# Conditioned decoder layer in fp32 on one core: the conditioning vector is loaded first and the sum of squares moves into the modulation

## The chip, the cores and the metric

The kernel runs on 1 core of one Trainium2 chip. The metric is the device time of one execution in microseconds (us); the median of three runs of the kernel before is 2164.31 us. Five engines matter here: TensorE (PE) multiplies, VectorE (DVE), ScalarE (ACT) and GpSimd (POOL) do elementwise work, SyncE (SP) issues most of the loads. SP and ACT each feed one hardware DMA queue; both queues are served by the same 16 DMA engines.

## The reference, cut to what matters

One layer for 320 tokens (256 of a prompt, 8 samples of 8 tokens), width 4096, weights in float32. The part that the change touches is the head of it:

```
mod = c @ w_ada + b_ada                       # c: 9 conditioning vectors of 4096, w_ada: 4096 x 12288
shift, scale, gate = split(mod, 3)
h = x * rsqrt(mean(x*x) + EPS) * g_norm * (1 + scale) + shift
proj = h @ w_in                               # then convolutions, RG-LRU, S5, GLU
x = x + gate * (mixed @ w_out)                # and a final RMSNorm
```

So each group of 4 x 128 channels of h needs three things: 1/rms of x (one number per token, over all 4096 channels), that group's shift, and that group's scale.

## The kernel before, in words

Each engine runs one program, ordered by semaphores; there is no scheduler. Everything is channel-major: x is held as 32 tiles of 128 channels x 320 tokens (5 MB).

**The modulation.** `w_ada` comes in slabs of 512 KB (two 128 x 512 tiles). 16 slabs make one part (512 output columns: shift or scale), two parts make one group j, and the first four groups (8 parts, 128 slabs) are worked through before the first projection: this is `with pe.Fori(0, ADA_1)`, lines 404 to 411. For each slab `ada_slab` (line 393) multiplies it by `c`, which is the stationary operand (CT, 32 columns). One slab shows as 4 MATMUL records of line 393. After a part, ACT copies the sums out of PSUM (`acc_copy`, line 576), and PE turns them to channel-major by `ada_sum` (line 401). Slab numbers in this document count from 0 over the whole stage: part 0 of group 0 is slabs 0 to 15, its part 1 slabs 16 to 31.

**The ring.** SP loads the slabs into a ring of 8 slots: 8 at once (line 299), and then slab n as soon as PE has used slab n - 8 (`ada_used`, line 303). After the 120th refill SP issues the first four slabs of `w_in` (line 307) and the next ring of `w_ada` (line 313).

**The sum of squares.** ACT issues x first and then 13 small loads on its own queue (lines 539 to 548), among them c, and six of these share the semaphore `small_in`. When all are issued ACT squares x in 8 pieces (line 555), DVE adds them up (lines 850, 853), and PE sums over the partitions with four matmuls against ones (line 386), 8 records in the trace. PE does this first of all; the modulation stands behind it in PE's program.

**The chain behind the sum.** ACT takes the root (line 559), then begins the preparation of the S5 coefficients together with DVE: exp (563), products (860, 861), exp (565), softplus and range reduction (864 to 872), exp (568), two sines (570, 571), and on DVE the softplus series (876 to 885). Only behind these stands DVE's reciprocal that makes 1/rms (line 888, `rstd_done`). In ACT's program `acc_copy` of group 0 stands behind the two sines. PE's program waits for `rstd_done` at the end of part 0 of every group, ahead of `ada_sum`, and no slab of part 1 is used before that:

```
                    if part == 0:
                        pe.wait_ge(rstd_done, 1)
                    ada_sum(j, part)
```

DVE goes on with the S5 preparation up to line 918 (`bb_ready`), then makes the first group of h (lines 927 to 944, with ACT's line 580). `ada_sum` of group j also waits until h of group j - 1 is written (`ht_done`).

**After the stage.** The projections follow, 3 matmuls of 320 columns per weight tile (lines 375 to 377), in 56 blocks, with the rest of `w_ada` between them; then the recurrences, the output projection and the final norm. Nothing there is touched by the change.

Of the kernel before, what the change touches and what calls it, by code (L numbers as in the profile page):

```python
# [30 lines left out]
T = TP + DB * DS  # L31
# [8 lines left out]
SPG = KT // 2  # L40
# [18 lines left out]
ADA_1 = ADA_J // 2  # L59
# [45 lines left out]
def build(nc, a):  # L105
    ctx = ExitStack()
    with ctx:
        def sem(name):

            return ctx.enter_context(nc.semaphore(name))  # L110
# [4 lines left out]
        def at(name, off, *shape, dt=F32):  # L115
            n = int(np.prod(shape))
            assert off + n <= WORDS, name
            t = nc.alloc_sbuf_tensor_at(name, [P, *shape], dt, offset=ORIGIN + 4 * off)
            return t
# [3 lines left out]
        def take(n):  # L123
            nonlocal o
            start = o
            o += -(-n // 8) * 8
            return start
# [16 lines left out]
        CT = at("c_T", o_ct, KT, 32)  # L144
        PAR = at("par", take(N_PAR), N_PAR)
        SELONES = at("sel_ones", take(9 + P), 9 + P)
        SEL, ONES = SELONES[:, 0:9], SELONES[:, 9:9 + P]
        o_s5h0 = take(512)
        S5H0 = at("s5_h0", o_s5h0, NST, 2, DB)
        o_cb = take(384)  # L150
        CBST = at("convb_state", o_cb, 16, DB, 3)
        LRU0 = at("lru_h0", take(128), 16, DB)
# [15 lines left out]
        SQA = at("x_sqa", o_h + 14 * REP + 8 * T, 4 * T)  # L168
# [68 lines left out]
        A0 = [ctx.enter_context(nc.psum_tensor(f"aux{i}", [P, 512], F32)) for i in range(4)]  # L237
# [6 lines left out]
                          for k, n, width in (("part_c", 2, SW), ("part_b", 4, XW)))  # L244


        small_in, x_in, s5_in = sem("small_in"), sem("x_in"), sem("s5_in")
        w_landed = [sem(f"w_landed{i}") for i in range(RING)]
        ada_landed = [sem(f"ada_landed{i}") for i in range(2 * RING)]
        adax_landed = [sem(f"adax_landed{i}") for i in range(RING)]  # L250
# [5 lines left out]
        sq_done, sqa_done, sum_done, root_done, rstd_done = map(  # L256
            sem, ["sq_done", "sqa_done", "sum_done", "root_done", "rstd_done"])
# [102 lines left out]
        def _(pe):  # L360
            mm = nc.tensor.matmul
# [18 lines left out]
                last.then_inc(slab_done, 1)  # L380


            pe.wait_ge(small_in, 16 * 6)
            pe.wait_ge(sqa_done, 8)
            for i in range(4):
                last = mm(A0[3][:, 0:T], ONES, SQA[:, i * T:(i + 1) * T], start=i == 0, stop=i == 3)  # L386
            last.then_inc(sum_done, 1)

            def ada_slab(part, sl, slot):
                for kk in range(2):  # L390
                    k = 2 * sl + kk
                    r = 32 * (k % 4)
                    last = mm(A0[part][r:r + 32, :], CT[:, k, :], slot[:, kk, :], start=k < 4, stop=k >= KT - 4)  # L393
                last.then_inc(ada_used, 1)

            def ada_sum(j, part):

                pe.wait_ge(acc_out, 2 * j + part + 1)
                pe.wait_ge(ht_done, j + 1)
                for b in range(BLK):  # L400
                    last = mm(A0[2 + part][:, 9 * b:9 * b + 9], ACCS[:, b * P:(b + 1) * P], SEL, start=True, stop=True)
                last.then_inc(sel_done, 1)

            with pe.Fori(0, ADA_1) as j:
                for part in range(2):
                    for sl in range(SPG):
                        pe.wait_ge(ada_landed[sl % 8], 64 * j + 32 * part + 16 * (sl // 8 + 1))
                        ada_slab(part, sl, ADA[:, sl % 8])
                    if part == 0:
                        pe.wait_ge(rstd_done, 1)  # L410
                    ada_sum(j, part)


            with pe.Fori(0, ADA_J - ADA_1) as jj:
# [18 lines left out]
            with pe.Fori(0, N_A) as u:  # L433
                for c in range(SPG):
                    slab(SLAB_A + u * SPG, c, KT, Q_A + u, H_HI, H_LO, T)
                    if c in (1, 3, 6, 9):
                        j = c // 3
# [4 lines left out]
                        for n in range(2):  # L442
# [3 lines left out]
                            last = mm(out, BBU_LO[r, n, :], UU_HI[r, :], start=False, stop=True)  # L446
                        last.then_inc(bu_done, 1)
                    if c in (8, 15):
# [5 lines left out]
                        for n in range(2):  # L454
                            for par in range(2):
                                j = 2 * pair + par
                                last = mm(A0[2][32 * j:32 * j + 32, 0:SW], CC[:, n, j, :], HRI[par][:, n, :],
                                          start=n == 0, stop=n == 1)
# [9 lines left out]
            with pe.Fori(0, N_B // 2) as i:  # L468
                for c in range(SPH):
                    slab(SLAB_B + i * SPB, c, KT // 2, Q_B + 2 * i, H_HI, H_LO, T, k0=KT // 2)  # L470
                for c in range(SPG):
                    slab(SLAB_B + i * SPB + SPH, c, KT, Q_B + 2 * i + 1, H_HI, H_LO, T)
                    if c in (5, 11):
# [5 lines left out]
                        for hd in range(2):  # L479
                            for w in range(2):  # L480
                                last = mm(A0[2 * w + hd][:, 0:XW], WG[:, 2 * pr + hd, w, :],  # L481
                                          XB[:, 2 * pr + hd, :], start=True, stop=True)
# [5 lines left out]
            with pe.Fori(0, N_O) as j:  # L488
                n = 0
                for c in range(SPG):  # L490
# [3 lines left out]
                    for _ in range(per[c]):  # L494
                        pe.wait_ge(gate_landed[n % RING], 64 * j + 16 * (n // RING + 1))
                        for kk in range(2):
                            k = 2 * n + kk
                            r = 32 * (k % 4)
                            last = mm(A0[0][r:r + 32, :], CT[:, k, :], ADA2[:, n % RING, kk, :], start=k < 4,  # L499
                                      stop=k >= KT - 4)  # L500
                        last.then_inc(gate_used, 1)
                        n += 1
                    if c == 13:
                        pe.wait_ge(gacc_out, j + 1)
                        pe.wait_ge(gmod_done, j + 1)
                        for b in range(BLK):
                            last = mm(A0[1][:, 9 * b:9 * b + 9], ACC2[:, b * P:(b + 1) * P], SEL, start=True,
                                      stop=True)
# [6 lines left out]
        def _(act):  # L515
# [20 lines left out]
                    act.wait_ge(slab_done, nb_next + 1)  # L536


            act.dma_start(X[:], a["x"]).then_inc(x_in, 16)
            for dst, name in ((CT, "c"), (PAR, "par"), (SELONES, "sel_ones"), (S5H0, "s5h0"), (LRU0, "lru"),  # L540
                              (CAST, "ca")):
                act.dma_start(dst[:], a[name]).then_inc(small_in, 16)
            for i in range(3):
# [19 lines left out]
            fn(T0[2][:], T0[2][:], ACT.Exp).then_inc(s5_act, 1)  # L563
            act.wait_ge(s5_dve, 2)
            fn(T0[6][:], T0[6][:], ACT.Exp).then_inc(s5_act, 1)
            act.wait_ge(small_in, 16 * 6)
            act.wait_ge(s5_dve, 3)
            fn(NEG8SP[:], NEG8SP[:], ACT.Exp).then_inc(s5_act, 1)
            act.wait_ge(s5_dve, 4)
# [67 lines left out]
            with act.Fori(0, 2) as h:  # L637
                st.enter(h, 32)
                for m in range(4):
# [3 lines left out]
                    for c in range(AHEAD, AHEAD + SPG):  # L643
# [8 lines left out]
                        if c in (3, 6, 9, 12):  # L652
                            j = c // 3 - 1
# [10 lines left out]
                        if c in (6, 9, 12, 15):  # L664
                            j = c // 3 - 2
# [145 lines left out]
            for g in range(FIN_DVE, ADA_J):  # L811
                for b in range(BLK):
                    k = 4 * g + b
                    act.wait_ge(fin_pool, k - 4 * FIN_DVE + 1)
                    last = fn(X[:, k, :], X[:, k, :], ACT.Copy, scale=PAR[:, C_GF + k:C_GF + k + 1])
# [4 lines left out]
        def _(dve):  # L820
# [15 lines left out]
            def col(c):  # L836

                return PAR[:, bass.ds(c, 1)] if not isinstance(c, int) else PAR[:, c:c + 1]
# [20 lines left out]
            dve.wait_ge(s5_act, 1)  # L859
            tt(ANG[:], IM[:], DT[:], MUL)  # L860
            tt(MAG[:], RE[:], DT[:], MUL).then_inc(s5_dve, 1)
            dve.wait_ge(small_in, 16 * 6)
            lam = PAR[:, C_LAM:C_LAM + 16]
            then(ts(SPT[:, 0], lam, -1.0, None, MUL))
            then(tt(SPT[:, 1], SPT[:, 0], lam, ALU.max))
# [315 lines left out]
            for g in range(FIN_DVE):  # L1181
                for b in range(BLK):
                    k = 4 * g + b
                    last = stt(X[:, k, :], X[:, k, :], col(C_GF + k), RST2[:], MUL, MUL)  # L1184
# [243 lines left out]
```

## Time and profile before

| | |
|---|---|
| median of 3 runs | 2164.31 us (2162.28 to 2164.57) |
| span of the profiled execution | 2165.0 us |
| PE busy over the span | 2033.5 us (94%) |
| DVE, ACT, POOL busy | 1053.5, 801.1, 437.0 us |
| first matmul of the program | 37.42 us |
| first matmul of the modulation | 41.82 us |
| last slab of the stage | 201.10 us |

The page gives the span only; no own time of the profiled execution beside it is listed. Its span lies 0.7 us above the median of the runs, so nothing that matters lies outside it. All moments below are microseconds from the start of the span. In the timeline a row is start, duration, engine, line, what, count, and in brackets how long the engine was idle before and what released it.

### The profile page before, as it was taken

The numbers are of one execution on the slowest core, as the hardware profiler recorded it, in microseconds if no ns is written. First come the engines' busy times: TensorE is split into PE (matmuls) and PEld (weight loads), VectorE is DVE, ScalarE is ACT, GpSimd is POOL, SyncE is SP. The second block draws the span as 40 slices with busy tenths as digits, with TensorE's granted clock in tenths as the row PEclk, the third lists the DMA queues.
The fourth block names the chain that finished last, engine by engine and source line by source line (L and its number), as shares of the span: only waits on it lengthen the run. The fifth ranks groups of instructions, "written<-read, shape, count | busy, mean of one in ns | idle before, by whom it ended". The sixth has DMA issues, their size and how long they took to land.

```text
span 2165.0 us, 36787 instructions
## 1 busy us (share of the span) xinstructions
PE 2033.5 (94%) x13066; PEld 1729.1 (80%) x13066; DVE 1053.5 (49%) x1324; ACT 801.1 (37%) x1075; POOL 437.0 (20%) x501
## 2 busy tenths in 40 slices
PE   2787999999999998999988999999999999999994
PEld 0112777778999988899988999999978887888883
DVE  4812233334446787666876456555643333333234
ACT  3001232233244444444444464745733222333222
POOL 0000000000008765687657000000000000000001
PEclk9999999999999999999999999999999999999997
DMA  8999999997443333433334535444386678666862
GB/s 319 410 410 378 339 340 354 339 336 281 148 146 129 129 109 126 134 128 128 120 120 139 171 129 177 152 153 170 107 322 219 227 273 301 231 222 223 300 223 97
DMA packets 129150, 473.89 MB, mean 219 GB/s; under 512 B 14640, under 2 KB 15472, under 8 KB 128960
## 3 DMA queue, kind: packets, MB, share of 16 engines
q1 hardware_dynamic: 122256, 445.70, 57.6%
q0 software_dynamic: 4816, 18.10, 2.4%
q10 hardware_dynamic: 2016, 9.42, 1.1%
q8 instruction: 20, 0.33, 0.1%
q14 instruction: 42, 0.34, 0.1%
HBM read 463.09 MB, written 10.07 MB: 219 GB/s over the span
## 4 chain that ended last, share of the span: by engine, by line
PE 75%; POOL 7%; DMA 7%; issue 4%; DVE 4%; ACTq 1%; ACT 1%; POOLq 0%; SPq 0%; DVEq 0%
PE m L375 22%; PE m L377 21%; PE m L376 21%; DMA ada_ring<-in_ada 6%; PE aux L499 4%; PE aux L393 4%; POOL s_tmpp L1257 1%; POOL s_tmpp L1260 1%; PE aux L481 1%; POOL sin L1216 1%; DVE x L1184 1%; POOL s_h__105 L1256 1%; POOL cos L1218 1%; DMA ada_ring_x<-in_ada 1%; DVE w_lo L833 1%
## 5 line engine op out<-in xcount | busy, mean ns | idle before, releaser
L375 PE MATMUL m<-h_hi,w_hi 128*128 128x320 f32 x3584 | 1134.8, 317 | 4.8 <-DVE w_lo L833 4.8
L377 PE MATMUL m<-h_hi,w_lo 128*128 128x320 f32 x3584 | 1110.0, 310 | 0.0
L376 PE MATMUL m<-h_lo,w_hi 128*128 128x320 f32 x3584 | 1109.6, 310 | 0.0
L833 DVE TENSOR_TENSOR w_lo<-w_raw,w_hi 128x1024 fp32r<-128x1024 f32 x456 | 578.8, 1282 | 866.0 <-ACT w_hi L529 864.9
L529 ACT ACTIVATE w_hi<-w_raw 128x1024 fp32r<-128x1024 f32 x456 | 479.4, 1057 | 929.3 <-PE m L377 604.9
L375 PEld LDWEIGHTS m<-h_hi,w_hi 128*128 128x128 f32 x3584 | 675.5, 188 | 150.6 <-issue 126.2
L376 PEld LDWEIGHTS m<-h_lo,w_hi 128*128 128x128 f32 x3584 | 676.0, 189 | 0.8
L377 PEld LDWEIGHTS m<-h_hi,w_lo 128*128 128x128 f32 x3584 | 675.4, 188 | 0.0
L393 PE MATMUL aux<-ada_ring,c_T 128*32 128x512 f32 x512 | 121.9, 613 | 24.7 <-DMA ada_ring<-in_ada 24.7
L393 PEld LDWEIGHTS aux<-ada_ring,c_T 128*32 128x32 f32 x512 | 17.5, 108 | 122.8 <-DMA ada_ring<-in_ada 119.3
L499 PE MATMUL aux<-gate_ring,c_T 128*32 128x512 f32 x512 | 93.1, 605 | 1.7 <-DMA gate_ring<-in_ada 1.7
L393 PE MATMUL aux<-ada_ring_x,c_T 128*32 128x512 f32 x512 | 70.3, 612 | 3.6 <-DMA ada_ring_x<-in_ada 3.6
L1309 POOL DMA_DIRECT2D x<-in_x x8 | 4.3, 534 | 330.5 <-PE m L377 330.5
L1226 POOL DMA_DIRECT2D part_b<-part_b x4 | 2.4, 590 | 339.5 <-ACT part_b L605 339.5
L1313 POOL TENSOR_TENSOR x<-x,rstd 128x320 f32<-128x320 f32 x8 | 8.6, 1111 | 235.9 <-DVE rstd L1179 235.9
L1300 POOL COPY stage_h<-lru_r 128x18 f32<-128x18 f32 x8 | 4.9, 616 | 240.7 <-DVE lru_r L1094 240.7
L576 ACT ACTIVATE ada_acc<-aux 128x512 f32<-128x512 f32 x16 | 9.5, 594 | 115.9 <-PE aux L393 115.9
L1256 POOL TENSOR_TENSOR s_h__104<-q,cos 128x328 f32<-128x328 f32 x16 | 19.7, 1233 | 155.1 <-DVE q L1007 155.1
L1219 POOL TENSOR_TENSOR sin<-sin,cos 128x328 f32<-128x328 f32 x34 | 43.4, 1278 | 6.0 <-POOL cos L1218 5.9
L628 ACT ACTIVATE cos<-sin 128x328 f32<-128x328 f32 x33 | 15.7, 475 | 70.7 <-POOL sin L1219 70.6
L386 PE MATMUL aux<-x_sqa,sel_ones 128*128 128x320 f32 x8 | 4.5, 740 | 37.4 <-DVE x_sqa L853 37.4
L1260 POOL TENSOR_TENSOR s_tmpp<-q,cos 128x328 f32<-128x328 f32 x32 | 36.3, 1136 | 0.0
(237 smaller groups left out, 1520.4 us busy)
## 6 DMA issues: line engine op xcount, KB each, us to landing
w_raw<-in_w SPq DMA_DIRECT2D x456, 512.0 KB, 4.3
ada_ring<-in_ada SPq DMA_DIRECT2D x128, 512.0 KB, 9.0
ada_ring_x<-in_ada SPq DMA_DIRECT2D x128, 512.0 KB, 5.9
gate_ring<-in_ada SPq DMA_DIRECT2D x128, 512.0 KB, 5.2
x<-in_x ACTq DMA_DIRECT2D x1, 5120.0 KB, 16.6
x<-in_x POOLq DMA_DIRECT2D x8, 640.0 KB, 5.9
out_y<-x SPq DMA_DIRECT2D x7, 640.0 KB, 2.9
part_b<-part_b POOLq DMA_DIRECT2D x4, 688.0 KB, 6.2
```

The lines of the kernel that those rows point to most:

```text
L375: mm(out, w_hi, hi[:, k, :], start=k == k0, stop=False)
L376: mm(out, w_hi, lo[:, k, :], start=False, stop=False)
L377: last = mm(out, w_lo, hi[:, k, :], start=False, stop=k == k0 + nk - 1)
L393: last = mm(A0[part][r:r + 32, :], CT[:, k, :], slot[:, kk, :], start=k < 4, stop=k >= KT - 4)
L481: last = mm(A0[2 * w + hd][:, 0:XW], WG[:, 2 * pr + hd, w, :], XB[:, 2 * pr + hd, :], start=True, stop=True)
L499: last = mm(A0[0][r:r + 32, :], CT[:, k, :], ADA2[:, n % RING, kk, :], start=k < 4, stop=k >= KT - 4)
L529: fn(W_HI[:, c % RING], RAW[:, c % RING].rearrange("p (k n) -> p k n", k=2), ACT.Copy).then_inc(w_hi_done, 1)
L833: tt(W_LO[:, c % RING], RAW[:, c % RING].rearrange("p (k n) -> p k n", k=2), W_HI[:, c % RING].bitcast(F32), SUB).then_inc(w_lo_done, 1)
L1184: last = stt(X[:, k, :], X[:, k, :], col(C_GF + k), RST2[:], MUL, MUL)
L1219: tt(sin, sin, cos, SUB).then_inc(frac_done, 1)
L1256: tt(hr, qr, cos, MUL)
L1260: then(tt(TMPP[:], qi, cos, MUL))
```

## The change

PE no longer begins with the sum of squares. c is loaded first on ACT's queue and has a semaphore of its own; PE waits for it and starts on slab 0. The first of the four groups is written out ahead of the loop (now over groups 1 to 3), and in it, behind slab 13 of part 0, PE waits for the small loads and for the last addition of squares, and does the four matmuls with ones. Nothing else moves; the chain behind the sum is the same.

```
-            pe.wait_ge(small_in, 16 * 6)
-            pe.wait_ge(sqa_done, 8)
-            for i in range(4):
-                last = mm(A0[3][:, 0:T], ONES, SQA[:, i * T:(i + 1) * T], start=i == 0, stop=i == 3)
-            last.then_inc(sum_done, 1)
+            def x_sum():
+
+                pe.wait_ge(small_in, 16 * 5)
+                pe.wait_ge(sqa_done, 8)
+                for i in range(4):
+                    last = mm(A0[3][:, 0:T], ONES, SQA[:, i * T:(i + 1) * T], start=i == 0, stop=i == 3)
+                last.then_inc(sum_done, 1)
...
-            with pe.Fori(0, ADA_1) as j:
+            def ada_alone(j, first):
                 for part in range(2):
                     for sl in range(SPG):
                         pe.wait_ge(ada_landed[sl % 8], 64 * j + 32 * part + 16 * (sl // 8 + 1))
                         ada_slab(part, sl, ADA[:, sl % 8])
+                        if first and part == 0 and sl == SPG - 3:
+                            x_sum()
                     if part == 0:
                         pe.wait_ge(rstd_done, 1)
                     ada_sum(j, part)
+
+            pe.wait_ge(c_in, 16)
+            ada_alone(0, True)
+            with pe.Fori(1, ADA_1) as j:
+                ada_alone(j, False)
...
+            act.dma_start(CT[:], a["c"]).then_inc(c_in, 16)
             act.dma_start(X[:], a["x"]).then_inc(x_in, 16)
-            for dst, name in ((CT, "c"), (PAR, "par"), (SELONES, "sel_ones"), (S5H0, "s5h0"), (LRU0, "lru"),
+            for dst, name in ((PAR, "par"), (SELONES, "sel_ones"), (S5H0, "s5h0"), (LRU0, "lru"),
                               (CAST, "ca")):
```

The waits of ACT and DVE on `small_in` go from six loads to five as well.

## Rows read from the trace of the kernel before

**Rows 1.** The page: the span in 40 slices, of 54 us each.

```profile
PEclk9999999999999999999999999999999999999997
DMA  8999999997443333433334535444386678666862
```

**Rows 2.** Stretches: us, busy time of PE, PEld, DVE, ACT, POOL, then PEclk, DMA share, GB/s.

```profile
30.00:35.00 5.00, 0.00 (x0) 0.00 (x0) 4.69 (x4) 4.03 (x4) 0.00 (x0) 1.00 1.02 408
35.00:40.00 5.00, 2.58 (x5) 1.82 (x6) 2.17 (x2) 1.68 (x2) 0.00 (x0) 1.00 0.12 43
40.00:45.00 5.00, 5.00 (x36) 1.64 (x35) 0.11 (x1) 2.90 (x3) 0.00 (x0) 1.00 0.16 51
...
60.00:80.00 20.00, 15.86 (x68) 2.68 (x67) 19.76 (x14) 0.60 (x1) 0.00 (x0) 0.91 1.03 409
```

**Rows 3.** Timeline, 20 to 60 us: from ACT's last issue to slab 16.

```profile
20.88 1.54 ACTq L548 DMA_DIRECT2D s_step<-in_step  x1
...
37.42 4.46 PE L386 MATMUL aux<-x_sqa,sel_ones 128*128 128x320 f32 x8 [37.42 <-DVE x_sqa L853]
...
41.82 3.64 PE L393 MATMUL aux<-ada_ring,c_T 128*32 128x512 f32 x32
41.93 0.53 ACT L559 ACTIVATE rstd<-aux,eps 128x320 f32<-128x320 f32 x1 [5.23 <-PE aux L386]
...
51.21 1.05 PE L393 MATMUL aux<-ada_ring,c_T 128*32 128x512 f32 x4 [0.21 <-DMA ada_ring<-in_ada]
...
56.34 1.05 PE L393 MATMUL aux<-ada_ring,c_T 128*32 128x512 f32 x4 [0.22 <-DMA ada_ring<-in_ada]
...
56.98 2.15 DVE L888 RECIPROCAL rstd<-rstd 128x320 f32<-128x320 f32 x1
57.52 0.60 ACT L576 ACTIVATE ada_acc<-aux 128x512 f32<-128x512 f32 x1 [1.56 <-PE aux L393]
...
59.37 1.05 PE L401 MATMUL aux<-sel_ones,ada_acc 128*128 128x9 f32 x8 [1.98 <-DVE rstd L888]
60.35 2.19 PE L393 MATMUL aux<-ada_ring,c_T 128*32 128x512 f32 x16
```

**Rows 4.** Timeline, 60 to 215 us: slab 27, first h, last slab, end of stage.

```profile
73.10 1.05 PE L393 MATMUL aux<-ada_ring,c_T 128*32 128x512 f32 x4 [0.23 <-DMA ada_ring<-in_ada]
...
96.44 1.27 ACT L580 ACTIVATE h_hi<-h_tmp 128x1280 f32 x1 [16.44 <-DVE h_tmp L941]
...
99.89 0.60 ACT L576 ACTIVATE ada_acc<-aux 128x512 f32<-128x512 f32 x1 [2.18 <-PE aux L393]
...
201.10 1.05 PE L393 MATMUL aux<-ada_ring,c_T 128*32 128x512 f32 x4 [0.23 <-DMA ada_ring<-in_ada]
...
207.50 3.17 PE L393 MATMUL aux<-ada_ring_x,c_T 128*32 128x512 f32 x8 [3.59 <-DMA ada_ring_x<-in_ada]
```

**Rows 5.** DMA issues, 0 to 60 us: KB each, median us from issue to landing.

```profile
x<-in_x ACTq DMA_DIRECT2D x1, 5120.0 KB, 16.6
c_T<-in_c ACTq DMA_DIRECT2D x1, 512.0 KB, 18.7
```

**Rows 6.** DMA queues, 0 to 60 us: packets, MB, share (q1 is SP's, q10 ACT's).

```profile
q10 hardware_dynamic: 2016, 9.42, 39.6%
```

**Rows 7.** DMA issues, 2.1 to 2.2 us, 6.2 us, and 42.0 to 43.3 us.

```profile
ada_ring<-in_ada SPq DMA_DIRECT2D x1, 512.0 KB, 15.8
ada_ring<-in_ada SPq DMA_DIRECT2D x1, 512.0 KB, 24.9
ada_ring<-in_ada SPq DMA_DIRECT2D x1, 512.0 KB, 3.2
```

**Rows 8.** DMA queues, 2.5 to 10 us, then 17.5 to 25 us.

```profile
q10 hardware_dynamic: 65, 2.66, 84.6%
q1 hardware_dynamic: 40, 0.16, 5.3%
...
q1 hardware_dynamic: 621, 2.28, 74.9%
q10 hardware_dynamic: 615, 0.79, 28.6%
```

**Rows 9.** Stretches around the two times that PE stands still.

```profile
66.00:68.00 2.00, 2.00 (x10) 0.21 (x6) 1.93 (x3) 0.00 (x0) 0.00 (x0) 0.50 1.04 414
205.00:210.00 5.00, 2.50 (x8) 0.38 (x8) 4.59 (x10) 1.28 (x2) 0.00 (x0) 0.55 0.59 234
```

**Rows 10.** The chain that ended last: start, us, what; eight full-clock fp32 records.

```profile
1260.22 2.31 PE aux L481 x8
```

More of the change, by code:

```diff
@@ L244, in build @@
                           for k, n, width in (("part_c", 2, SW), ("part_b", 4, XW)))
-        small_in, x_in, s5_in = sem("small_in"), sem("x_in"), sem("s5_in")
+        small_in, c_in, x_in, s5_in = sem("small_in"), sem("c_in"), sem("x_in"), sem("s5_in")
         w_landed = [sem(f"w_landed{i}") for i in range(RING)]
@@ L565, in _ @@
             fn(T0[6][:], T0[6][:], ACT.Exp).then_inc(s5_act, 1)
-            act.wait_ge(small_in, 16 * 6)
+            act.wait_ge(small_in, 16 * 5)
             act.wait_ge(s5_dve, 3)
@@ L861, in _ @@
             tt(MAG[:], RE[:], DT[:], MUL).then_inc(s5_dve, 1)
-            dve.wait_ge(small_in, 16 * 6)
+            dve.wait_ge(small_in, 16 * 5)
             lam = PAR[:, C_LAM:C_LAM + 16]
```

## The prediction

> **What bounds the kernel now.** I read the page first, slice by slice: the DMA engines are nine tenths busy or more through the first four slices, about 216 us, and only half busy later [rows 1]. So the head of the kernel, where `w_ada` streams in, is set by the loads, and the rest by TensorE. Whatever the change does, it does in the head; what follows depends on it through one moment only, the end of the stage, and shifts with it as a block.
>
> Then the stretches of the head. The loads run at 408 GB/s to 35 us, nearly stop for two stretches (share 0.12 and 0.16), and run at full share afterwards [rows 2]. The hole is 5 x 0.88 + 5 x 0.84 = 8.6 us. The timeline says why: all 8 ring slots are full, PE does not touch them before 41.82 us because the sum of squares stands ahead in its program, starts at 37.42 and takes 4.46 us, and ACT could only begin to square when its last issue was out at 22.42 us (20.88 + 1.54) [rows 3]. This hole is what the change can win.
>
> The same timeline shows a second place. PE stands still at the end of part 0 until line 401 at 59.37, released by the reciprocal of line 888 [rows 3]. That reciprocal ends a chain which begins when the sum is done, at 37.42 + 4.46 = 41.88. The chain is therefore 59.37 - 41.88 = 17.5 us long. In the kernel before PE needs 57.4 us for its first 16 slabs anyway (56.34 + 1.05), so only 2 us of the chain are seen. From slab 27 at 73.10 to slab 127 at 201.10 it is 128.0 us for 100 slabs, 1.28 us each, every one released by its load [rows 4]: in this stretch a shift at slab 27 arrives whole at the end of the stage.
>
> **The change part by part.** One slab is 0.524 MB, 1.28 us.
>
> *c ahead of x, own semaphore.* c landed 18.7 us after its issue because it stood behind x; x took 16.6 us for 5 MB [rows 5]. Now c lands within a few us and x about 1.3 us later (0.52 MB at 408 GB/s). Neither is on the path: PE's first slab landed at about 2.1 + 15.8 = 17.9 us, also behind x [rows 7]. The reason is in the queues: from 2.5 to 10 us ACT's queue moved 2.66 MB in 65 packets and SP's only 0.16 MB in 40 [rows 8], so x with its 41 KB packets takes nearly everything. PE will begin at about 18 us, not at 4. The squares end at about 37.4 us, within 1.5 us of before, since ACT's issues are paced by the same queue; they are needed only behind slab 13. Cost 0; if that cover went, a late square would delay the chain one for one, and it has some 7 us to spare.
>
> *Modulation first.* As slab 0 is used at about 19 us, the refills follow at once and the hole at 36 us closes: slab 8 need not wait until 43. Gain to that point 8.6 us.
>
> *When is slab 13 there?* Before, 9.42 MB of ACT's queue [rows 6] and 8 slabs (4.19 MB) were through at about 35.6 us (the 0.12 of the stretch from 35 us) [rows 2]. Six slabs more are 3.15 MB, 7.7 us at 408 GB/s: 43.3 us. About 1 us goes from last byte to use, and the last small loads (0.3 MB, 0.8 us) may come behind: 44.0 us. Bounds: 45 us if all small loads win; and 40.2 us if SP's queue kept the 75% share of the stretch from 17.5 to 25 us [rows 8] from slab 0 on (18 + 13 x 0.524 / 0.306). I take 44.0: after that stretch ACT's queue carries rows of 4 KB like SP's own, and the two should share about evenly.
>
> On this point the Trainium skill (DMA: Bandwidth & Descriptors, Queues, rings and completion order) says that each DMA engine goes round the queues that have work, one packet at a time. The trace agrees for x (41 KB against 4 KB a turn, shares 84.6% and 5.3%) [rows 8]; by that rule slab 13 comes at 44, while a constant 75% share would put it at 40.2 and the forecast 3.8 us lower.
>
> A second rule speaks against the sum. The Trainium skill (same page, Specifications) gives 358 GB/s as the limit of HBM for one core. By it the 3.15 MB would take 8.8 us, and the forecast would be 1.1 us higher; the trace has 408 to 414 GB/s over whole stretches [rows 2, 9], and the measurement decides.
>
> *The sum inside the stage.* Behind slab 13 (44.0 + 1.0 for its matmuls) stand the 8 records. Before they ran after 37 us of idleness and took 4.46 us [rows 3]; eight fp32 records of a little more columns take 2.31 us in a busy stretch [rows 10], so the former is the 1.2 GHz level. In the stretch from 66 us the clock was 0.50 after PE had been standing and starting again [rows 9], so either level is possible here. I take 2.3, with 4.5 as upper bound, because the slabs now keep PE working from 18 us on. The sum is done at 44.0 + 1.0 + 2.3 = 47.3 us, 5.4 us later than before. The 2.3 us themselves are covered by the ring.
>
> *The chain behind it* is unchanged in work and order: 17.5 us. All its other inputs are there by then. `ada_sum` of part 0 starts at 47.3 + 17.5 = 64.8 us, not 59.37, and slab 16 at 64.8 + 1.0 = 65.8, not 60.35 [rows 3]. Slabs 14 and 15 are done by 48.5. So PE stands for about 16 us. Queued behind it are all slabs of part 1, and behind them SP's refills, which wait for `ada_used`.
>
> *Does the ring cover that?* Slabs 16 to 23 are in the ring or in flight at 48.5 and are in by 44.0 + 10 x 1.28 = 56.8 us. From there the loads have nothing to do until PE resumes at 65.8. The hole has moved from 36 us to 57 us.
>
> *The restart.* Before, from 41.82 (eight slabs full, loads idle, the same state) to slab 11 at 51.21 it was 9.4 us [rows 3]; the first refill landed 3.2 us after its issue [rows 7]. Slab 27 now stands where slab 11 stood. After 16 us of standing PE will be at 1.2 GHz: at 207.5 us, after 3.6 us of standing, two slabs took 3.17 us and the clock of the stretch was 0.55 [rows 4, 9], whereas before the restart the sum had warmed it up. That delays the first refill by about one cold slab more, 0.8 us (bounds 0 and 1.5). Slab 27: 65.8 + 9.4 + 0.8 = 76.0 us, against 73.10 [rows 4].
>
> *The sum:* 76.0 - 73.1 = +2.9 us. All gain of 8.6 us is given back and a little more.
>
> *Peeled group, a longer program for PE:* no row prices it. Its cover is the ring (each PE stand of 2 us at the ends of parts costs nothing between slab 27 and 127); 0, at most 1.4 us. That bound is what the loads fell behind their step between slab 15 at 56.34 and slab 27 at 73.10: 16.76 us less 12 x 1.28 = 15.4, at full share [rows 3, 4, 2].
>
> *DVE and ACT later:* the S5 preparation ends 5.4 us later, so h of group 0 goes from 96.44 + 1.27 = 97.7 to 103.1 on ACT, in front of `acc_copy` of the next part, which before came at 99.89 [rows 4] and would be due at 102.8. PE waits 0.3 us more there, under the ring's cover. Cost 0.
>
> Forecast: 2164.3 + 2.9 = 2167.2 us. The sum was made in the profiled execution (2165.0), where it would give a span of about 2167.9.
>
> **The rivals.**
>
> A. *The sum runs at 1.2 GHz, or slab 13 comes late.* Same mechanism as the forecast, but the sum is done at 49.5 instead of 47.3, so +5.1 us, 2169.4; with slab 13 at 45 and the instruction loads' 1.4 us 2171.8. It is slower by over 0.2% once the sum ends later than 48.7 us. For it: clock 0.50 at 66 us and the 4.46 us. Against it: many loosely spaced slabs from 50 to 56 us took the same 1.05 us as later at full clock.
>
> B. *The ring hides the chain; faster.* If the part-0 wait cost no load time, the whole 8.6 us would stay: 2155.7. The place is line 401 of part 0. The loads can bridge a stand of about 7 us (8 slabs of 1.28 less the 3.2 us restart), so it would need the reciprocal before about 55.5 us, that is, a sum done by 38 us. The squares are only there at 37.4 and slab 13 at 40.2 at the earliest, so the trace speaks against it. Half a success (sum done at 43.5, slab 13 at 40.2) gives -0.9 us, 2163.4, which is within no change.
>
> C. *The change does not do what it says: nothing moves.* If PE were held at slab 0 for longer, or the ring refilled no sooner, the sum would again come first in effect and the time be 2164.3. Against it: slab 0 landed at 17.9, slab 7 at 6.2 + 24.9 = 31.1 us [rows 7], all before the old start.
>
> **How the numbers follow.** 0.2%, 4.3 us, is about what a measurement of this kernel can tell from no change. The forecast and the small cases on its two sides (half of B, C): 0.53. A: 0.37, which takes in the mixed cases with one term at its upper bound. B: 0.10, for a chain that overlaps in a way I do not see. The predicted time is that of the forecast, 2167.2. Range: upwards to A with nearly everything at its bound, 2171.5; downwards past half of B, 2160.5, leaving B outside. The likeliest case's own range is 2163.4 to 2168.6.
>
> **What the profile of the changed kernel would show.** First matmul of line 393 at about 18 us. Load share full from 5 us to about 56 us, then a hole of some 10 us or more ending near 67 us. The records of ones behind slab 13 at about 45 us, 2.3 or 4.5 us long. Line 888 about 17 us behind them, PE's line-401 idle there about 16 us, released by DVE. Slab 27 near 76.0, last slab of the stage near 204.0. The prediction is wrong if the chain behind the sum is shorter than 17.5 us in the new order, if slab 13 is there before 41 us, or if the loads do not pause near 57 us.

## The result, and the profile after

| | before | changed |
|---|---|---|
| median of 13 runs | 2164.14 us (2162.11 to 2166.0) | 2167.96 us (2165.6 to 2170.75) |
| ratio | | 1.0018, 95% interval 1.001 to 1.0026 |

The change makes the kernel slower by 3.8 us, a difference that the interval separates from zero but that stays under the 0.2% (4.3 us) of the prediction. Ratios count fast runs alone, and one slow run, at 4937.28 us, of the kernel with the sum behind slab 11 is left out.

The stretches of the changed kernel, columns as in [rows 2], show the time without loads (the hole) at its new place:

```profile
35.00:40.00 5.00, 3.46 (x12) 0.33 (x8) 0.43 (x1) 0.00 (x0) 0.00 (x0) 0.71 1.03 409
40.00:45.00 5.00, 3.48 (x16) 0.43 (x12) 0.00 (x0) 0.00 (x0) 0.00 (x0) 1.00 1.03 407
...
50.00:55.00 5.00, 0.00 (x0) 0.00 (x0) 4.39 (x8) 2.47 (x4) 0.00 (x0) 0.66 1.03 409
55.00:60.00 5.00, 0.00 (x0) 0.00 (x0) 4.83 (x7) 0.98 (x2) 0.00 (x0) 0.50 0.14 55
60.00:65.00 5.00, 0.23 (x1) 0.23 (x2) 4.55 (x17) 2.02 (x3) 0.00 (x0) 0.50 0.01 2
65.00:70.00 5.00, 5.00 (x26) 2.35 (x30) 4.90 (x5) 0.00 (x0) 0.00 (x0) 0.50 0.09 20
70.00:75.00 5.00, 4.34 (x28) 0.95 (x20) 4.93 (x5) 0.00 (x0) 0.00 (x0) 0.80 0.99 362
```

The two stretches in which the loads nearly stopped [rows 2] now run at full share. In their place three others are empty: 5 x (0.86 + 0.99 + 0.91) = 13.8 us without loads, against 8.6 before. PE is idle in the middle of them while DVE works.

Its timeline, to set beside [rows 3, 4]. Line numbers moved: the modulation is line 395, the ones 388, `ada_sum` 403, the reciprocal 898.

```profile
18.65 7.44 PE L395 MATMUL aux<-ada_ring,c_T 128*32 128x512 f32 x20 [18.65 <-DMA ada_ring<-in_ada]
19.10 1.47 ACTq L558 DMA_DIRECT2D s_step<-in_step  x1
...
44.07 1.05 PE L395 MATMUL aux<-ada_ring,c_T 128*32 128x512 f32 x4 [0.20 <-DMA ada_ring<-in_ada]
45.05 2.42 PE L388 MATMUL aux<-x_sqa,sel_ones 128*128 128x320 f32 x8
47.40 1.06 PE L395 MATMUL aux<-ada_ring,c_T 128*32 128x512 f32 x8
47.51 0.53 ACT L569 ACTIVATE rstd<-aux,eps 128x320 f32<-128x320 f32 x1 [12.67 <-PE aux L388]
...
62.56 2.15 DVE L898 RECIPROCAL rstd<-rstd 128x320 f32<-128x320 f32 x1
...
64.77 1.88 PE L403 MATMUL aux<-sel_ones,ada_acc 128*128 128x9 f32 x8 [16.30 <-DVE rstd L898]
...
66.57 7.76 PE L395 MATMUL aux<-ada_ring,c_T 128*32 128x512 f32 x40
...
76.87 1.05 PE L395 MATMUL aux<-ada_ring,c_T 128*32 128x512 f32 x4 [0.21 <-DMA ada_ring<-in_ada]
...
103.65 0.60 ACT L586 ACTIVATE ada_acc<-aux 128x512 f32<-128x512 f32 x1 [0.36 <-PE aux L395]
...
110.77 1.05 PE L395 MATMUL aux<-ada_ring,c_T 128*32 128x512 f32 x4 [0.86 <-DMA ada_ring<-in_ada]
...
205.48 1.05 PE L395 MATMUL aux<-ada_ring,c_T 128*32 128x512 f32 x4 [0.24 <-DMA ada_ring<-in_ada]
...
211.88 3.17 PE L395 MATMUL aux<-ada_ring_x,c_T 128*32 128x512 f32 x8 [3.60 <-DMA ada_ring_x<-in_ada]
```

Read it from the bracket of line 403: PE stood 16.30 us, released by the reciprocal (line 898), and it had finished slabs 14 and 15 at 48.46. Slab 127 starts at 205.48 instead of 201.10, and the first slab of the next ring at 211.88 instead of 207.50 [rows 4]: the stage ends 4.4 us later in both readings. The medians of the whole kernel differ by 3.8 us.

The span of this profiled execution (2164.2 us) is none the less below that of before (2165.0). The delay is made up far behind the change: the first matmuls of the S5 output come at 670.2 us against 666.7, the last at 1175.1 against 1173.7, and the first gate matmuls of the RG-LRU at 1260.7 against 1260.1. The same program varies by more than the effect: its 13 runs spread over 5.2 us, and the profiled one (2165.76 us) was the second shortest. So below I read the effect from slab 127, which ends the part that was changed, and set the timed ratio beside it.

### The profile page after: what moved, and what is told of

It is laid out like the page before. It is cut to its first block, busy times and chain, and to the rows that moved or that the text cites. A ratio compares the mean times of both kernels' runs of the same rounds, so it can differ in the third digit from the quotient of the medians.

```text
span 2164.2 us, 36780 instructions
## 1 busy us (share of the span) xinstructions
PE 2038.3 (94%) x13066; PEld 1728.5 (80%) x13066; DVE 1050.7 (49%) x1324; ACT 799.9 (37%) x1075; POOL 435.3 (20%) x501
## 4 chain that ended last, share of the span: by engine, by line
PE 75%; DMA 8%; POOL 7%; issue 4%; DVE 4%; ACT 1%; POOLq 0%; SPq 0%; DVEq 0%
PE m L375 22%; PE m L377 21%; PE m L376 21%; DMA ada_ring<-in_ada 7%; PE aux L508 4%; PE aux L395 4%; POOL s_tmpp L1270 1%; POOL s_tmpp L1267 1%; PE aux L490 1%; DVE x L1194 1%; POOL cos L1228 1%; POOL s_h__105 L1266 1%; POOL sin L1226 1%; DMA ada_ring_x<-in_ada 1%; DVE w_lo L843 1%
## 5 line engine op out<-in xcount | busy, mean ns | idle before, releaser
L395 PE MATMUL aux<-ada_ring,c_T 128*32 128x512 f32 x512 | 130.5, 696 | 44.9 <-DMA ada_ring<-in_ada 44.9
L403 PEld LDWEIGHTS aux<-sel_ones,ada_acc 128*128 128x128 f32 x128 | 16.6, 199 | 29.1 <-DVE rstd L898 17.2
```

## The experiments

My theory was that the sum's end, through the 17.5 us chain behind it, sets when PE resumes. Rivals were the load order, the longer program, interleaving as such, and a threshold of the ring. Each kernel below was timed between runs of the kernel before of its own, whose medians were 2163.33 to 2165.68 us; a ratio is against those, so medians of different runs are not to be set side by side. Each position in the trace comes from one profiled execution.

**The sum ahead of slab 0 again, all else as changed.**

```
-                        if first and part == 0 and sl == SPG - 3:
-                            x_sum()
...
             pe.wait_ge(c_in, 16)
+            x_sum()
             ada_alone(0, True)
```

> PE's order of before (the sum ahead of slab 0) in an otherwise changed kernel: c loaded first, group 0 written out. My theory: the loss comes from the late chain alone, so with the sum first again it goes. ACT's issues ended 1.85 us earlier in the changed kernel (c no longer behind x), so the sum should start at about 35.5 instead of 37.4, PE's line 403 of part 0 near 57.5, slab 27 near 71.2, slab 127 near 199.2, time about 2162.3 (-1.9 us against before). Rival: the written-out group or the order of the loads costs time; then slab 127 is at 203 or later and the time at 2166 or more.

Measured: line 403 of part 0 at 56.91 us, slab 127 at 199.14, median 2163.32 us, ratio 0.9993 (0.9984 to 1.0002). The loss is gone and 2.0 us are won in the head, as forecast; over the whole kernel that is not separable from no change. Neither the written-out group nor the load order makes the loss of 4.4 us; the next run shows what the written-out group costs.

**The load order alone.**

```
-            act.dma_start(X[:], a["x"]).then_inc(x_in, 16)
-            for dst, name in ((CT, "c"), (PAR, "par"), ...
+            act.dma_start(CT[:], a["c"]).then_inc(c_in, 16)
+            act.dma_start(X[:], a["x"]).then_inc(x_in, 16)
+            for dst, name in ((PAR, "par"), ...
```

> Only the load order of the change (c ahead of x, a semaphore of its own), the loop not written out. My theory: the same as the run with the sum first, slab 127 near 199.2, time about 2162.3. If the longer program of PE costs something, this run is faster than that one by it (my bound was 1.4 us).

Measured: line 402 of part 0 at 56.55, slab 127 at 198.50, median 2163.84, ratio 0.9992 (0.9983 to 1.0001). That is 0.6 us ahead of the run with the group written out, under my 1.4. One profile each could be chance, but the place is there: with the group written out one slab comes 0.95 us late behind line 403 of group 1, part 0 (2.23 us from 102.19 to 104.42, where a step is 1.28), and with the loop none does (128.0 us from slab 27 to 127). The account of the prediction below comes back to it.

**The place of the sum: behind slab 8, 11 or 15 instead of 13.**

```
-                        if first and part == 0 and sl == SPG - 3:
+                        if first and part == 0 and sl == SPG - 8:     # 8; for 11: SPG - 5; for 15: SPG - 1
```

> The changed kernel with the sum behind slab 8 instead of slab 13. My theory: the time follows the end of the chain one for one. Slab 8 is done at 36.4 us, the sum at 38.7 to 40.8 (either clock), but exp (line 573) must then wait for the last small load at about 42.7, so the chain starts there: line 403 at 58.4 us, slab 27 near 70.5, slab 127 near 199, time about 2161.6, faster than before. Rival (the loss comes from something else, such as the interleaving, cold clock or contention): slab 127 stays at 205.5 and the time near 2168.

> The changed kernel with the sum behind slab 11. My theory, one for one with the end of the sum: slab 11 starts at 41.1, the sum runs from 42.1 to 44.5, line 403 of part 0 at 61.9, slab 127 at 202.6 to 203.2, so 1.5 to 2 us behind the kernel before and 2.5 ahead of the changed one; time about 2166. Rival (a threshold: the ring covers the chain up to some place and then fails): either 198.5 as behind slab 8, or 205.5 as behind slab 13.

> The changed kernel with the sum behind slab 15. My theory: the sum is done at about 50.1 us instead of 47.5, so everything behind comes 2.7 us later: line 403 at 67.4, slab 127 near 208.1, time about 2170.6. Rival (place does not matter since PE has 16 us of standing time anyway): unchanged, 205.5 and 2168.

| sum behind slab | sum starts, us | line 403 of part 0 | slab 127 | against before | ratio (95%) |
|---|---|---|---|---|---|
| 8 | 36.03 | 57.80 | 198.49 | -2.6 | 0.9989 (0.998 to 0.9998) |
| 11 | 42.84 | 62.56 | 203.13 | +2.0 | 1.0005 (0.9996 to 1.0014) |
| 13 (the change) | 45.05 | 64.77 | 205.48 | +4.4 | 1.0018 (1.001 to 1.0026) |
| 15 | 47.53 | 67.24 | 208.81 | +7.7 | 1.0034 (1.0022 to 1.0047) |

From 11 to 15 the sum starts 4.69 us later and line 403 comes 4.68 us later; from 8 to 11 line 403 moves 4.76 us and slab 127 4.64 us: one for one along the chain, and no threshold. Slab 127 moves 5.68 us from 11 to 15, and 0.8 us of that are slabs that come late (1.5 us in all with the sum behind slab 15, 0.7 us behind slab 11). Behind slab 8 the chain waits for a load as well.

The rows of the run with slab 8, first PE's part of the timeline, then ACT's:

```profile
36.03 3.99 PE L388 MATMUL aux<-x_sqa,sel_ones 128*128 128x320 f32 x8
...
57.80 1.87 PE L403 MATMUL aux<-sel_ones,ada_acc 128*128 128x9 f32 x8 [10.33 <-DVE rstd L898]
```

```profile
42.39 1.09 ACT L573 ACTIVATE s5t<-s5t 128x1064 f32<-128x1064 f32 x1 [0.50 <-DMA s_step<-in_step]
```

The sum ends at 40.0 us, and from there to line 403 it is 17.8 us instead of the 17.3 of the change (64.77 - 47.47). The 0.5 us are what exp (line 573) waits for the last small load, as forecast: it starts at 42.39, while root and table load would have let it start at about 41.9. The sum itself took 3.99 us here (granted clock 0.60 from 36 to 40 us, so mostly the 1.2 GHz level) and 2.42 us behind slab 13 (1.00 from 45 to 48 us, the 2.4 GHz level).

**The sum done twice over.** The four matmuls are issued twice; the second pass overwrites the first.

```
+                for _ in range(2):
                     for i in range(4):
                         last = mm(A0[3][:, 0:T], ONES, SQA[:, i * T:(i + 1) * T], start=i == 0, stop=i == 3)
```

> The changed kernel with the four matmuls of the sum done twice over (the second time overwrites the first with the same numbers). PE has 16 us of standing time behind them. My theory: the sum's own duration lies on the chain, so 8 more records (2.1 us at full clock) move line 403 of part 0 from 64.8 to 66.9 and slab 127 from 205.5 to about 207.6. Rival: hidden in the standing time, nothing moves.

Measured in one profile: the 16 records took 4.57 us, line 403 at 66.83 (+2.06), slab 127 at 208.46 (+3.0); the one time is 2172.48 us. PE had 16 us to spare behind the sum, and still its 2.1 us arrive in full: what matters is when the sum ends, not how busy PE is. The further 0.9 us arise behind line 403 and were not expected: 0.4 of them lie between line 403 and slab 27 (12.46 us against 12.10), the rest in one slab that comes 1.20 us late instead of 0.63.

**The chain cut short.** DVE takes the reciprocal first, ACT copies the sums of part 0 right behind the root; ACT's loop over the groups is written out.

```
+            acc_copy(0, 0)                      # ACT, behind the root
...
+            dve.wait_ge(root_done, 1)
+            nc.vector.reciprocal(RSTD[:], RSTD[:]).then_inc(rstd_done, 1)
             dve.wait_ge(s5_act, 1)
             tt(ANG[:], IM[:], DT[:], MUL)
...
-            dve.wait_ge(root_done, 1)
-            nc.vector.reciprocal(RSTD[:], RSTD[:]).then_inc(rstd_done, 1)
```

> The changed kernel with the chain cut short: DVE takes the reciprocal of the root ahead of its S5 preparation, ACT does the first copy of the sums right behind the root. My theory: the hole near 57 us goes, line 403 of part 0 comes near 50.5 us; but h of group 0 still waits for the whole S5 preparation on DVE and ACT (about 102 us), and PE's line 403 of group 1 part 0, now due at 89, must wait for it until about 103. The hole moves there (98 to 107 us) and slab 59 lands near 114.6 against 114.1 before: slab 127 near 201.6, time about 2164.7, no change against before. Rival: the chain in front of the reciprocal was the only limit, and this run gains the whole 8.6 us, 2155.7, slab 127 near 192.5.

Measured: slab 127 at 201.64, median 2164.34, ratio 1.0005 (0.9996 to 1.0014). PE's part of the timeline:

```profile
50.12 1.70 PE L403 MATMUL aux<-sel_ones,ada_acc 128*128 128x9 f32 x8 [1.81 <-DVE rstd L874]
...
102.82 1.87 PE L403 MATMUL aux<-sel_ones,ada_acc 128*128 128x9 f32 x8 [13.31 <-ACT ada_acc L574]
```

and the stretches:

```profile
50.00:95.00 45.00, 34.41 (x144) 7.58 (x144) 42.47 (x52) 6.53 (x8) 0.00 (x0) 0.85 1.03 409
95.00:105.00 10.00, 2.18 (x12) 1.98 (x16) 6.71 (x15) 1.75 (x2) 0.00 (x0) 0.50 0.20 78
105.00:110.00 5.00, 5.00 (x32) 1.03 (x24) 1.99 (x5) 0.00 (x0) 0.00 (x0) 0.66 0.46 156
```

The stand at part 0 shrank from 16.30 to 1.81 us, and a new one of 13.31 us appeared at the next part 0, where h of group 0 is late; 10.7 us without loads (10 x 0.80 + 5 x 0.54). In ACT's program the copy of the sums stands behind h of group 0, and h behind the S5 preparation. The first wait only hid the second.

**The chain cut short, and h of group 0 taken ahead.** As above; DVE modulates group 0 behind its long reciprocal, in the middle of the S5 preparation, and splits it afterwards; ACT's first copy of group 1 goes before h of group 0. DVE's loop over the groups is written out too.

```
             nc.vector.reciprocal(U1[:, w], U1[:, w])
+            dve.wait_ge(rstd_done, 1)
+            h_tmp(0)
+            h_rows(0)                           # up to ht_done; the split into H_LO is now h_low(j)
...
+            acc_copy(0, 1)                      # ACT
+            acc_copy(1, 0)
+            act.wait_ge(bb_ready, 1)
+            h_hi(0)
+            acc_copy(1, 1)
```

> As the run with the early root, and h of group 0 is modulated by DVE in the middle of its S5 preparation (behind the long reciprocal), its split into two parts left behind; ACT does the first copy of group 1 before h of group 0. My theory: now no stand of PE outlasts the ring, the loads run without a hole from 2 us on, slab 127 at 191 to 193 instead of 201.1 before, time about 2155.5 (-8.6 us, ratio 0.996). Rival: the loads themselves cannot run through (contention of the two queues, one more hole at a later part), so the gain stays under 4 us.

Measured: slab 127 at 190.77, 10.3 us before the kernel before; median 2153.91, ratio 0.9957 (0.9944 to 0.9971). Its stretches:

```profile
5.00:55.00 50.00, 26.86 (x104) 5.59 (x104) 16.96 (x16) 17.17 (x16) 0.00 (x0) 0.93 1.02 411
55.00:70.00 15.00, 11.06 (x46) 1.85 (x44) 14.25 (x28) 3.98 (x5) 0.00 (x0) 1.00 1.03 409
70.00:190.00 120.00, 98.57 (x426) 18.29 (x426) 44.79 (x62) 6.79 (x8) 0.00 (x0) 1.00 1.03 409
```

The loads run through from 5 to 190 us. In the changed kernel the middle one of these stretches has a share of 0.08. The same kernel once more, beside the next one:

> The kernel with the early root and the early h once more, on the chip and between the same runs of the kernel before as the one with PE's order of before, so that the two can be compared: slab 127 at 190.8, time 2154 to 2156.

It gave slab 127 at 190.77 again, median 2152.97, ratio 0.9948 (0.9935 to 0.9961).

**The short chain with PE's order of before.** The last kernel with the sum ahead of slab 0.

> The kernel with the early root and the early h, but with PE's order of before: the sum ahead of slab 0. It asks what PE's new order is worth once the chain is short. My theory: each of the two is worth something only with the other; the hole from 35 to 42 us comes back (6.3 us without loads in the run with the sum first), slab 127 at 190.8 + 6.3 = 197.1, time about 2160.5. Rival (the shorter chain alone gives the gain, the order of PE nothing): slab 127 at 191, time 2154.

Measured: slab 127 at 198.66, median 2162.39, ratio 0.9983 (0.9975 to 0.9992). Its stretches:

```profile
35.00:40.00 5.00, 4.68 (x16) 2.79 (x20) 0.17 (x1) 0.48 (x1) 0.00 (x0) 1.00 0.05 19
40.00:45.00 5.00, 4.05 (x36) 0.79 (x24) 2.15 (x1) 0.05 (x1) 0.00 (x0) 1.00 0.66 224
```

The hole is back: 5 x (0.95 + 0.34) = 6.5 us. Slab 127 is 7.9 us later than without it, 1.6 more than I had written. So PE's new order is worth 7.9 us in the head, but only on top of a short chain; the short chain alone is worth 0.5 us against the run with the sum first (199.14).

## Why the prediction was right, point by point

Predicted 2167.2 us, measured 2167.96. The path held: the hole is closed, the chain behind the sum opens a larger one, and its end sets the time. Two terms of the sum were too small and one was right for a reason that the rows do not bear out; the medians happen to lie closer to the forecast (0.8 us) than the end of the stage does (1.5 us).

- *The bound.* Loads in the head, a shift of the whole block behind it: confirmed. Once ACT's loads are through and outside the holes, the slabs of every kernel come 1.28 us apart, but for one or two late ones each (below).
- *c ahead of x.* PE's first slab at 18.65 (forecast about 18), behind x and not behind c, which landed 3.9 us after its issue. The squares ended sooner than forecast: ACT's last issue was out at 20.57 us instead of 22.42, since c no longer waits behind x. I had costed this at 0; it is worth about 2 us where the sum is not tied to a slab (the two runs with PE's order of before).
- *Slab 13.* Forecast 44.0, measured 44.07. The sum over both queues' bytes carried it, but the hit is closer than its terms: 43.3 and 1.0 make 44.3 already, and the last small load landed at 42.6 (19.10 + 23.5), ahead of slab 13, the case for which the prediction had 45. The turn-by-turn rule of the Trainium skill (DMA: Bandwidth & Descriptors, Queues, rings and completion order) agrees: from 18 to 42 us SP's queue moved 1726 packets and ACT's 1665. The turns were even, the bytes were not (6.28 and 3.57 MB). The constant 75% share (40.2) is refuted. So is the same page's 358 GB/s (Specifications) as a price for this core, which loads alone: the stretches of 120 us and more without a hole show 408 and 409.
- *The sum.* It took 2.42 us (forecast 2.3), the full clock, so rival A's first condition did not come about; it ended at 47.47 (47.3). The reason given, that the slabs keep PE working from 18 us on, did not hold: the granted clock was 0.61 from 30 to 35 us and 0.71 from 35 to 40, and it was back at 1.00 only from 40 us. Behind slab 8 the sum still ran mostly at the lower level. Here the forecast had some luck.
- *The chain.* Line 403 at 64.77 (64.8); PE stood 16.30 us (about 16).
- *The restart.* This term was too small. I allowed 0.8 us for an engine at half clock. `ada_sum` itself took 1.88 instead of 1.05 us, so slab 16 started at 66.57 instead of 65.8, and from there to slab 27 it was 10.3 us instead of 9.4. Together 1.7 us: slab 27 at 76.87, not 76.0. The first part is the clock (0.50). The second is not shown to be the clock alone: behind slab 8 the same way took 9.5 us, after a stand of 10.33 us and at 0.50 and then 0.69.
- *Between slab 27 and 127.* 128.6 us instead of 128.0; I had 0 for the written-out group, with 1.4 as bound. The 0.6 us lie in one slab, at 110.77 instead of 110.14. Sum: +4.4 in the head where I said +2.9 (0.9 from the restart, 0.6 from here), +3.8 in the medians.
- *Side costs.* h of group 0 late on ACT: `acc_copy` of group 1 at 103.65, line 403 at 104.37, 1.9 us behind the last slab as in the kernel before. No loss there, as forecast.
- *Rival B* (the ring hides the chain) is refuted by the places: behind slab 8 PE still stood 10.33 us and the two stretches from 55 us have load shares of 0.16 and 0.45. Its bridge of about 7 us was too long as well: stands of 10.33 us (slab 8), 13.31 (the chain cut short) and 16.30 (the change) left 7.0, 10.7 and 13.8 us without loads, so the ring hid 2.5 to 3.4 us of each. *Rival C* is refuted by slab 0 at 18.65. *Rival A* asked for a later end of the sum, and that did not come; what came on top of the forecast lay behind line 403.

The late slab deserves a look, because it comes with the written-out group. From slab 27 to slab 127 it is 128.0 us in the two kernels whose loop is whole (the kernel before and the one with the load order alone), and 128.6 to 129.5 us in seven of the others. In these seven one slab comes late while the load share stays full:

| kernel with group 0 written out | late slab starts, us | late by |
|---|---|---|
| the change | 110.77 | 0.63 |
| the sum first | 104.42 | 0.95 |
| sum behind slab 8 | 103.77 | 1.40 |
| sum behind slab 11 | 108.41 | 0.52 |
| sum behind slab 15 | 112.81 | 1.51 |
| the sum twice | 112.47 | 1.20 |
| short chain, sum first | 103.94 | 0.63 |

Each time one packet of 0.02 MB of a queue that the profile calls "instruction" ran 2 to 4 us before it, about 3 us behind line 403 of group 1, part 0: in the changed kernel between 107.7 and 108.4 us. The two kernels with the loop whole have no such packet there. They have one at group 0, as all have, and in the kernel before slabs 20 and 21 came 1.4 us behind the step of the loads next to it (packets at 60.8 to 63.1 us, late slabs at 63.73 and 65.42); in the changed kernel that packet ran in the hole and cost nothing.

What stays open: that the packet makes the slab late is a coincidence in time and not shown by a run of its own. In the kernel without holes such a packet ran at 93.6 to 94.4 us and no slab was late, while one at 53.0 to 53.8 us stood before a slab 1.0 us late, all that this kernel lacks between slab 13 (43.84) and 127 (190.77) against 114 steps of 1.28; and in the run with the chain cut short a slab at 113.31 is 0.6 us late with no such packet near. Nor does a run isolate the restart's second part.

## What to carry to other kernels

When a step is moved off the front of a queue to close a hole, follow what hangs on its result, not what it costs: here 2.4 us of PE work carried a 17 us chain through two other engines, and moving it 5.6 us later gave back 8.6 us and more. Look at the second wait as soon as the first is named: it had cost 2 us only because the first hid it, and a third one stood behind that. A ring covers less of a stand than its slots suggest (here 8 steps of 1.28 us hid about 3 us), and what goes beyond costs full time; if the work on the chain that nobody waits for yet (here the S5 preparation) is put behind the work that somebody does, the same change turns from +0.2% to -0.4%.

## What the hardware showed that I had not expected

- After the 16.3 us stand the granted clock stayed at 0.50 for the stretch from 65 to 70 us, in which PE was busy all 5.00 us, and 0.80 in the next. Eight records of 9 columns took 1.88 us instead of 1.05. Slab 27 came 1.7 us later behind the stand than with the times of the kernel before; 0.8 us of that is the lower clock, the rest is open.
- PE fell to the 1.2 GHz level without a long stand: from 30 to 35 us the clock was 0.61 with two slabs at gaps of 1.58 and 1.51 us. These rows are of the changed kernel:

```profile
29.25 1.05 PE L395 MATMUL aux<-ada_ring,c_T 128*32 128x512 f32 x4 [1.58 <-DMA ada_ring<-in_ada]
...
31.81 1.92 PE L395 MATMUL aux<-ada_ring,c_T 128*32 128x512 f32 x4 [1.51 <-DMA ada_ring<-in_ada]
```

  The four records of a slab took 1.05 us in the first and 1.92 us in the second. It cost nothing here, since the next slab was not yet there.
- The order in which ACT issues its loads changed when ACT came free: its third `rep` load held the queue until 16.4 us with x first and until 12.0 us with c first; its squares began 1.86 us earlier (21.89 against 23.75) with the same number of loads.
